# A mixture-of-experts decoder step on one core: a fifth expert weight buffer, separate waits for each weight, and three moved pieces of work

## The chip, the cores and the metric

The kernel runs on one core of a Trainium2 chip. The metric is the time of one execution on the device in microseconds (us). Everything is in 32-bit floating point.

## The reference, cut to what matters

One layer is computed for 320 tokens of width D = 1024: a prompt of 256 tokens and 8 samples of 8 tokens.

```python
xn = rmsnorm(x, norm1);  proj = xn @ w_in
# mixer 1: causal conv + RG-LRU scan       mixer 2: RWKV-7, 16 heads of 64
merged = sigmoid(gate_lru) * out_lru + sigmoid(gate_rwkv) * out_rwkv
x = x + merged @ w_out
# new_shift = P[:, -1]: the last row of the 3360 RWKV columns of each of the 9 sequences is an output
t = rmsnorm(x, norm2)
# router: best of 4 groups, then the best 2 of its 8 experts, softmax weights
h = silu(t @ wg[e]) * (t @ wu[e])          # 32 experts, wg and wu 1024 x 256
y = sum over the two experts of weight * (h @ wd[e])   # wd 256 x 1024
out = rmsnorm(x + y, final_norm)
```

The three matrices of an expert are 1 MB each, so the 32 experts read 100.7 MB. The kernel visits all of them, with at most 64 tokens each (more go to an overflow loop, which does not run here).

## The kernel before, in words

Each engine runs its own program in order; semaphores join them. SP (SyncE) issues nearly all loads, in the order written and each behind its waits.

**Turns.** The two mixers are done in eight turns (`turn(i, first, last)`), one for each pair of heads. TensorE's program in a turn is the chain of the RWKV-7 chunk products: `level_w(k)` and `level_x(k)` for k = 1 to 5, each of which waits for a VectorE step. Between the levels stand halves of the next turn's projections (`ahead`). In the last turn there is no next turn, so only the projection `gl` is left of them, and in the other places TensorE only waits. Single products and projections share two PSUM banks, `bank[0]` and `bank[1]`, alternately: `room` makes TensorE wait until the product two before has been taken by ScalarE or VectorE. The order of these products in a turn is a list (`FULL`, `LAST`).

**Between the turns and the experts.** `out(t)` multiplies by `w_out` for three tiles of tokens; `x2(t)` transposes the normalised rows, and `logits(t)` makes the router's logits (signal `lg_ps`). Then TensorE transposes the 27 chunks of `lastP`, the nine shift-state rows, in groups of four into two banks, and ScalarE copies each group to `rowP` and stores it (lines 904 to 912 and 1229 to 1235). VectorE meanwhile finds group and experts (ending with `Mk`), then waits for ScalarE's exponentials, which stand behind the copies of the shift state, computes the gates (lines 1644 to 1649), waits for TensorE's counts of tokens for each expert (`cnt_ps`, lines 915 to 922), and computes slots and the index lists `gidx` (gather) and `sidx` (scatter). Before the index product TensorE also waits for the last copy of the shift state. GpSimd waits for both lists and starts the gathers of the experts' tokens from `xn2d`.

**Experts.** For each expert TensorE does GU (gate and up, 32 matrix instructions), T (8 transposes of the next expert's gathered tokens), DN (down, of the expert before), and one transpose of the hidden values. Weights lie in four buffers. One semaphore `ew{j}` counts all three loads of buffer j, and GU waits for all three. SP reloads gate and up of a buffer when its GU has ended (`gu`) and down when its DN has ended (`dn`):

```python
with sp.Fori(1, NE // 4) as i:
    for j in range(4):
        weights(j, i * 4 + j, f"ew{j}", i * 4 + (j - 3))
```

Experts 0 to 3 are loaded ahead: 0 and 1 behind the input loads, 2 behind `wo_ps` 3 (the end of `out(2)`), 3 behind the stores of the shift state. On TensorE, ScalarE and VectorE the loop is a first pass of four experts, a hardware loop, and on TensorE and ScalarE a last pass written out. GU also stands behind the arrival of the next expert's gathered tokens.

**End.** SP waits for the last scatter, loads the two results of each token (`ya`, three tiles, two loads each) and, after the first tile's, `final_norm` broadcast to 128 partitions; VectorE combines the tiles and scales them by `final_norm`, ScalarE makes the roots, SP stores.

## Time and profile before

| what | value |
|---|---|
| median of 3 runs | 911.65 us (909.9 to 912.21) |
| the profiled execution | 912.9 us, of which 911.0 us are the span of its trace |
| busy share of the span | PE 88%, PE weight loads 56%, DVE 50%, ACT 28%, POOL 7% |
| turns, `out`, router | 0 to about 618 us |
| experts | about 618 to 884 us |
| end | about 884 to 911 us |
| HBM read | 155.99 MB |

PE is TensorE, DVE is VectorE, ACT is ScalarE, POOL is GpSimd; SPq and ACTq are the queues from which SyncE and ScalarE issue transfers. The busy share of PE is an average over stages with different limits. The granted clock is the share of full speed that TensorE's clock had.

### The profile page before, as it was taken

Reading aid. Unit: us, or ns where it says so; the run is one execution under the profiler, and the core shown is the slowest. Engines: PE = TensorE matmul, PEld = TensorE weight load, DVE = VectorE, ACT = ScalarE, POOL = GpSimd, SP = SyncE. Lnnn points to the kernel's source line nnn. Section 1 sums busy time; section 2 is a strip of 40 time slices with the busy share of each in tenths; the row PEclk is TensorE's granted clock in tenths of the full one; section 3 lists DMA queues with packets and bytes.
Section 4 is the critical chain, followed back from the end, with each engine's and each line's share of the span. In section 5 each row is a group of like instructions: output and inputs, shape, how many; then the busy total and the mean of one; then the engine's idle time right before and its main releaser. Section 6 shows DMA issues by size and latency. Waiting matters only on the chain.

```text
span 911.0 us, 16423 instructions
## 1 busy us (share of the span) xinstructions
PE 800.2 (88%) x6090; PEld 510.3 (56%) x6090; DVE 459.5 (50%) x1067; ACT 250.9 (28%) x585; POOL 66.7 (7%) x74
## 2 busy tenths in 40 slices
PE   3999999999999999999999799957997887877860
PEld 3566666666766666666667564444554554544530
DVE  2476586786785875867867644351111111111115
ACT  4223351441432423514414222321111111111102
POOL 1000000000000000000000000002332222222110
PEclk9999999999999999999999799956999999999995
DMA  9451060250230500602502206755999999999925
GB/s 222 105 145 25 24 170 9 59 140 23 77 98 23 155 20 23 169 7 57 140 23 63 100 26 228 283 218 177 347 393 399 396 398 402 400 391 398 391 80 193
DMA packets 112633, 159.31 MB, mean 175 GB/s; under 512 B 27232, under 2 KB 91290, under 8 KB 104394
## 3 DMA queue, kind: packets, MB, share of 16 engines
q1 hardware_dynamic: 96580, 148.62, 47.3%
q0 software_dynamic: 5296, 6.19, 2.4%
q10 hardware_dynamic: 10727, 4.09, 1.8%
q8 instruction: 20, 0.33, 0.2%
q14 instruction: 10, 0.08, 0.0%
HBM read 155.99 MB, written 13.64 MB: 186 GB/s over the span
## 4 chain that ended last, share of the span: by engine, by line
PE 69%; DMA 17%; DVE 9%; issue 2%; ACT 1%; ACTq 1%; DVEq 0%; SPq 0%; POOL 0%; POOLq 0%
PE bank L591 17%; DMA vecs<-in_exp_down 8%; PE bank L943 8%; DMA wall<-in_exp_down 4%; PE bank L597 4%; PE bank L864 4%; PE bank L950 4%; PE bank L745 4%; PE bank L808 3%; PE bank L693 3%; DMA scratch<-in_exp_down 2%; PE bank L613 2%; PE bank L937 2%; PE bank L700 2%; DVE vecs L1360 2%
## 5 line engine op out<-in xcount | busy, mean ns | idle before, releaser
L591 PE MATMUL bank<-xnT,wall 128*128 128x320 f32 x656 | 197.3, 446 | 1.8 <-DVE wkv L1466 1.8
L591 PEld LDWEIGHTS bank<-xnT,wall 128*128 128x128 f32 x656 | 120.1, 191 | 52.2 <-DVE wkv L1466 5.4
L1705 DVE SCALAR_TENSOR_TENSOR vecs<-vecs,bank 128x128 f32<-128x128 f32 x32 | 9.2, 287 | 160.0 <-ACT vecs L1249 160.0
L943 PE MATMUL bank<-scratch 128*64 128x256 f32 x512 | 58.8, 382 | 19.0 <-DMA scratch<-in_exp_down 9.6
L943 PEld LDWEIGHTS bank<-scratch 128*64 128x64 f32 x512 | 40.3, 137 | 33.0 <-issue 19.8
L1699 DVE COPY vecs<-bank 128x512 f32<-128x512 f32 x32 | 22.1, 691 | 64.1 <-PE bank L950 64.1
L1249 ACT ACTIVATE vecs<-bank 128x128 f32<-128x128 f32 x32 | 8.9, 277 | 148.3 <-PE bank L943 148.3
L497 POOL DMA_INDIRECT merged<-xn2d,gidx x2 | 1.9, 942 | 613.6 <-DVE sidx L1693 613.3
L745 PE MATMUL bank<-xnT,wall 128*128 128x320 f32 x128 | 43.9, 455 | 2.5 <-DVE wkv L1506 2.5
L1459 DVE TENSOR_TENSOR wkv<-bank,consts_sb 128x256 f32<-128x256 f32 (+1 forms) x40 | 18.1, 451 | 48.4 <-PE bank L693 48.4
L943 PE MATMUL bank<-vecs,scratch 128*64 128x256 f32 x256 | 32.3, 409 | 8.8 <-DMA vecs<-in_exp_down 6.5
L943 PE MATMUL bank<-wall,scratch 128*64 128x256 f32 x256 | 31.1, 398 | 10.0 <-DMA wall<-in_exp_down 9.0
L503 POOL DMA_INDIRECT ybuf<-vecs,sidx x32 | 32.1, 1004 | 81.0 <-DVE vecs L1699 81.0
L693 PEld LDWEIGHTS bank<-wkv,scratch 64*64 64x64 f32 x704 | 24.4, 138 | 15.6 <-issue 13.3
L808 PE MATMUL bank<-xnT,wall 128*128 128x320 f32 x112 | 33.1, 439 | 0.0
L693 PE MATMUL bank<-wkv,scratch 64*64 64x64 f32 x704 | 30.0, 228 | 2.0 <-DVE wkv L1466 2.0
L950 PE MATMUL bank<-vecs 128*64 128x512 f32 x128 | 31.0, 605 | 0.4 <-ACT vecs L1256 0.4
L943 PEld LDWEIGHTS bank<-wall,scratch 128*64 128x64 f32 x256 | 21.3, 143 | 17.6 <-issue 11.0
L864 PE MATMUL bank<-wall,merged 128*128 128x512 f32 (+1 forms) x84 | 30.7, 595 | 0.1
L943 PEld LDWEIGHTS bank<-vecs,scratch 128*64 128x64 f32 x256 | 19.8, 147 | 19.0 <-issue 11.5
L1242 ACT ACTIVATE scratch<-bank 128x512 f32<-128x512 f32 x32 | 19.1, 597 | 40.3 <-PE bank L937 40.3
L700 PEld LDWEIGHTS bank<-wkv 64*64 64x64 f32 x576 | 20.2, 139 | 15.3 <-issue 12.7
(374 smaller groups left out, 1376.1 us busy)
## 6 DMA issues: line engine op xcount, KB each, us to landing
wall<-in_w_in SPq DMA_DIRECT2D x58, 512.0 KB, 5.5
vecs<-in_exp_down SPq DMA_DIRECT2D x16, 1024.0 KB, 18.7
scratch<-in_exp_gate SPq DMA_DIRECT2D x16, 1024.0 KB, 16.0
scratch<-in_exp_up SPq DMA_DIRECT2D x16, 1024.0 KB, 20.3
vecs<-in_exp_gate SPq DMA_DIRECT2D x8, 1024.0 KB, 15.5
vecs<-in_exp_up SPq DMA_DIRECT2D x8, 1024.0 KB, 19.9
scratch<-in_exp_down SPq DMA_DIRECT2D x8, 1024.0 KB, 18.3
wall<-in_exp_gate SPq DMA_DIRECT2D x8, 1024.0 KB, 16.3
```

The costliest lines, as they stand in the source:

```text
L503: pool.indirect_dma_start(yhalf, bass.IndirectOffsetOnAxis(ap=e, axis=0), ye[:, b, :], None, bounds_check=4 * QROWS - 1, oob_is_err=False) ...
L591: q = mm(tpbank(L, name), wbuf[name][:, k, :], xnT[:, k, :], start=(k == 0), stop=(k == KC - 1))
L597: mm(tpbank(L, name), lhsT, rhs, start=True, stop=True).then_inc(S("tp"), 1)
L693: q = mm(bank[2][at64(e), 64 * u:64 * u + 64], am[at64(e), u, e, 0, :], X[at64(e), u, :], start=True, stop=True)
L700: q = mm(bank[3][at64(e), 64 * u:64 * u + 64], Y[at64(e), u, :], W[at64(e), u, :], start=True, stop=True)
L745: q = mm(tpbank(L, "gr"), wbuf["gr"][:, k, :], xnT[:, k, :], start=(k == 0), stop=(k == KC - 1))
L808: q = mm(tpbank(L, "lx"), wbuf["lx"][:, k, :], xnT[:, k, :], start=(k == 0), stop=(k == KC - 1))
L864: q = mm(b, merged[:, k, t0:t0 + n], wo[k][:, 512 * h:512 * h + 512], start=(k == 0), stop=(k == KC - 1))
L943: q = mm(b[64 * f:64 * f + 64, 0:256], xT[:, k, :], w[:, :, k, 128 * f:128 * f + 128], start=(k == 0), stop=(k == KC - 1))
L950: q = mm(b[64 * d:64 * d + 64, :], hT[:, 64 * j:64 * j + 64], w[:, j, 512 * d:512 * d + 512], start=(j == 0), stop=(j == 1))
L1242: A(xgT[:, b], bank[b][:].rearrange("p (k s) -> p k s", k=KC), ACT.Copy).then_inc(S("gT"), 1)
L1699: CP(ye[:, j % 2, :], bank[6 + j % 2][:]).then_inc(S("ye"), 1)
```

## The change

- **A fifth buffer.** Five sets of gate and up (`wgu`) and of down (`wdn`, `dn4`) are laid over tiles that are dead at that time. The fifth down matrix lies in three pieces and is loaded by three transfers. Expert 3's gate and up wait for the stores of the shift state alone, expert 4's for the end of `out(2)`. Down of 1 waits for that too, down of 2 for the last `x2` and the stores of `xn2d`, down of 3 and 4 for `lg_ps`.
- **Own waits.** Gate and up of a buffer count on `ewg{b}`, down on `ewd{b}`. GU waits for the first, DN for the second. GU no longer waits for the next expert's tokens; the transposes T do.
- **Loops written out** on SP, TensorE, ScalarE and VectorE.
- **Shift-state rows in the last turn.** The 27 transposes of `lastP` become eight products `rows0` to `rows7` in the list `LAST`: six (four chunks each) at the places between the levels where TensorE only waited, and two (two chunks and one) between the last `level_x(4)` and the product `gx`. ScalarE copies them in between and issues the two stores ahead of the `gx` activation.
- **Gates behind the indices.** VectorE computes the five gate steps after `sidx`. GpSimd's first gathers wait for `gidx` alone.
- **`final_norm`** is loaded before the experts. The rows of the conv and LRU state are copied to another place and stored by eight transfers in place of four.

```diff
-LAST = Products([x for x in TURN if x[0] not in NEXT], AHEAD.order)
+ROWS = [(4 * g, 4 * g + 4) for g in range(6)] + [(24, 26), (26, 27)]
+OWN = [x for x in TURN if x[0] not in NEXT]
+LAST = Products(OWN[:2] + [(f"rows{g}", "a") for g in range(6)] + OWN[2:3] + [("rows6", "a"), ("rows7", "a")] + OWN[3:], AHEAD.order)
...
         wgu = [w.rearrange("p (g k f) -> p g k f", g=2, k=KC) for w in
-               (vecs[:, 0:4096], scratch[:, :], wall[:, 0:4096], scratch3[:, :])]
...
+               (vecs[:, 0:4096], vecs[:, 4096:8192], scratch[:, :], scratch3[:, :], wall[:, 0:4096])]
+        wdn = [scratch2[:, 0:2048], wall[:, 4096:6144], wkv[:, 3 * D:3 * D + 2048], xflat[:, 0:2048], None]
+        dn4 = [wkv[:, 5 * D:6 * D], mflat[:, 2048:2560], xflat[:, 2048:2560]]
...
@@ sync
+            load_gu(0, 0)
+            load_dn(0, 0)
+            load_gu(1, 1)
+            load_gu(2, 2)
+            sp.wait_ge(S("shift_out"), 32)
+            load_gu(3, 3)
             sp.wait_ge(S("wo_ps"), 3)
...
+            load_dn(1, 1)
+            load_gu(4, 4)
+            sp.dma_start(fnb, a["final_norm"].rearrange("(a d) -> a d", a=1).broadcast_to([P, D])).then_inc(S("fn_in"), 16)
+            sp.wait_ge(S("x2T_ps"), 6)
+            sp.wait_ge(S("xn2d"), 48)
+            load_dn(2, 2)
+            sp.wait_ge(S("lg_ps"), 1)
+            load_dn(3, 3)
+            load_dn(4, 4)
+            for e in range(5, NE):
+                sp.wait_ge(S("gu"), e - 4)
+                load_gu(e % 5, e)
+                sp.wait_ge(S("dn"), e - 4)
+                load_dn(e % 5, e)
...
@@ gpsimd
-            pool.wait_ge(S("idx"), 2)
+            pool.wait_ge(S("idx"), 1)
...
@@ tensor, in turn()
                     else:
+                        rows(2 * "rkv".index(n) + half)
                         needs()
+
+                def rows(g):
+
+                    room(L, i, f"rows{g}")
+                    for c in range(*ROWS[g]):
+                        w, at = min(P, RWKV - c * P), P * (c - ROWS[g][0])
+                        q = tr(bank[L.bank(f"rows{g}")][0:9, at:at + w], lastP[0:w, c, :], ident[0:w, 0:w])
+                    q.then_inc(S("tp"), 1)
...
+                if last:
+                    rows(6)
+                    rows(7)
                 pe.wait_ge(S("xc"), i + 1)
...
@@ tensor, experts
+            for e in range(NE + 1):
+                if e < NE:
+                    pe.wait_ge(S(f"ewg{e % 5}"), 32 * (e // 5 + 1))
+                    pe.wait_ge(S("gT"), e + 1)
+                    if e >= 2:
+                        pe.wait_ge(S("h"), e - 1)
+                    GU(bank[2 + e % 2], xgT[:, e % 2], wgu[e % 5]).then_inc(S("gu"), 1)
+                if e + 1 < NE:
+                    n = e + 1
+                    pe.wait_ge(S(f"xg{n % 4}"), 16 * (n // 4 + 1))
+                    T(bank[n % 2], xg[n % 4], n % 4 >= 2).then_inc(S("gT_ps"), 1)
+                if e:
+                    b = (e - 1) % 5
+                    pe.wait_ge(S("hT"), e)
+                    pe.wait_ge(S(f"ewd{b}"), (48 if b == 4 else 16) * ((e - 1) // 5 + 1))
+                    if e >= 3:
+                        pe.wait_ge(S("ye"), e - 2)
+                    DN(bank[6 + (e - 1) % 2], b).then_inc(S("dn"), 1)
+                if e < NE:
+                    pe.wait_ge(S("h"), e + 1)
                     tr(bank[4][:, 0:128], hh, ident).then_inc(S("hT_ps"), 1)
...
@@ scalar, in turn()
+            def rows(L, i, g):
+
+                c0, w = P * ROWS[g][0], min(P * ROWS[g][1], RWKV) - P * ROWS[g][0]
+                tp_ready(act, L, i, f"rows{g}")
+                A(rowP[:, c0:c0 + w], bank[L.bank(f"rows{g}")][0:9, 0:w], ACT.Copy).then_inc(S("taken_a"), 1)
```

## Rows read from the trace of the kernel before

**Rows 1.** The page's slices: GB/s in 40 slices of 22.8 us.

```profile
GB/s 222 105 145 25 24 170 9 59 140 23 77 98 23 155 20 23 169 7 57 140 23 63 100 26 228 283 218 177 347 393 399 396 398 402 400 391 398 391 80 193
```

**Rows 2.** Windows: span, busy us of PE, PEld, DVE, ACT, POOL, clock, DMA share, GB/s.

```profile
750.00:800.00 50.00, 39.61 (x284) 23.70 (x280) 7.60 (x18) 6.91 (x18) 11.03 (x12) 1.00 1.02 399
```

**Rows 3.** Timeline of PE, experts 0, 1, 9 and 31: start, us, work [idle before].

```profile
624.01 6.53 PE L943 MATMUL bank<-vecs,scratch 128*64 128x256 f32 x32 [0.78 <-DMA merged<-xn2d,gidx]
...
632.34 3.67 PE L943 MATMUL bank<-scratch 128*64 128x256 f32 x32 [0.46 <-ACT scratch L1242]
...
688.71 3.67 PE L943 MATMUL bank<-scratch 128*64 128x256 f32 x32 [2.10 <-DMA scratch<-in_exp_down]
...
874.90 3.67 PE L943 MATMUL bank<-scratch 128*64 128x256 f32 x32 [0.92 <-DMA vecs<-in_exp_down]
```

**Rows 4.** The chain that ended last, its end: start, us, what.

```profile
858.09 16.76 DMA vecs<-in_exp_down
...
878.57 1.72 PE bank L950 x8
...
880.97 1.96 PE bank L950 x8
```

**Rows 5.** Timeline of SP's queue: the issue of the last up matrix.

```profile
850.85 0.38 SPq L443 DMA_DIRECT2D scratch<-in_exp_up  x1
```

**Rows 6.** Transfers of 840 to 876 us: issues, KB each, us to landing.

```profile
scratch<-in_exp_up SPq DMA_DIRECT2D x1, 1024.0 KB, 17.7
```

**Rows 7.** Windows in the last turn, columns as in rows 2.

```profile
512.00:514.00 2.00, 0.58 (x18) 0.45 (x15) 1.93 (x5) 0.00 (x0) 0.00 (x0) 0.95 0.00 0
...
522.00:524.00 2.00, 2.00 (x6) 1.15 (x4) 0.00 (x0) 0.00 (x0) 0.00 (x0) 0.50 0.00 0
```

**Rows 8.** Timeline of PE in the last turn.

```profile
511.40 0.80 PE L700 MATMUL bank<-wkv 64*64 64x64 f32 x20 [1.01 <-DVE wkv L1459]
...
515.42 1.33 PE L700 MATMUL bank<-wkv 64*64 64x64 f32 x20 [0.59 <-DVE wkv L1459]
...
520.04 4.38 PE L591 MATMUL bank<-xnT,wall 128*128 128x320 f32 x8
...
524.96 2.42 PE L591 MATMUL bank<-xnT,wall 128*128 128x320 f32 x8
...
527.92 1.40 PE L597 MATMUL bank<-vecs,wxa 128*128 128x320 f32 x4
```

**Rows 9.** Timeline of PE in the router stage.

```profile
597.78 5.62 PE L910 MATMUL bank<-consts_sb,lastP 128*9 128x128 f32 x27
...
604.69 0.97 PE L921 MATMUL bank<-Mk,consts_sb 128*128 128x32 f32 x6
```

**Rows 10.** Timeline of ACT: one copy of a shift-state group.

```profile
598.84 0.59 ACT L1232 ACTIVATE scratch<-bank 9x512 f32<-9x512 f32 x1 [2.97 <-PE bank L910]
```

**Rows 11.** Timeline of DVE in the router stage.

```profile
603.01 0.26 DVE L1642 TENSOR_TENSOR Mk<-OH 128x96 f32<-128x96 f32 x1
606.15 0.17 DVE L1645 TENSOR_REDUCE r<-dg 128x3 f32<-128x12 f32 x1 [2.88 <-ACT r L1239]
...
607.22 0.14 DVE L1652 MEMSET slot<- 128x96 f32 x1
...
617.41 0.18 DVE L1691 CAST gidx<-tokf 64x41 uint32<-64x41 f32 x1
```

**Rows 12.** Timeline of POOL: the first gather.

```profile
618.24 0.96 POOL L497 DMA_INDIRECT merged<-xn2d,gidx  x1 [613.27 <-DVE sidx L1693]
```

**Rows 13.** Windows in the router stage, columns as in rows 2.

```profile
600.00:603.00 3.00, 2.98 (x16) 1.31 (x15) 2.56 (x15) 2.13 (x5) 0.00 (x0) 0.58 0.00 0
603.00:606.00 3.00, 2.66 (x21) 2.14 (x19) 0.26 (x1) 2.32 (x5) 0.00 (x0) 0.99 0.24 40
```

**Rows 14.** Timeline of the end: SP's queue and DVE.

```profile
887.71 0.43 SPq L474 DMA_DIRECT2D vecs<-in_final_norm  x1
...
898.17 1.28 DVE L1736 SCALAR_TENSOR_TENSOR wkv<-wall,r,wkv 128x1024 f32<-128x1024 f32 x1 [3.67 <-DMA scratch<-ybuf]
```

More of the change, by code:

```diff
@@ L437, in dn_src, with load_gu @@
                 return a["exp_down"][0].rearrange("e (j p) d -> p e j d", p=P)[:, bass.ds(e, 1)].rearrange("p e j d -> p (e j) d")
[L439 to L441 removed]
+            def load_gu(b, e):
                 for g, name in enumerate(("exp_gate", "exp_up")):
[L443 to L446 removed]
@@ L448, in _ @@
-            weights(0, 0, "ew0")
-            weights(1, 1, "ew1")
-            sp.wait_ge(S("wo_ps"), 3)
-            weights(2, 2, "ew2")
-            sp.wait_ge(S("shift_out"), 32)
-            sp.wait_ge(S("rows_out"), 64)
-            weights(3, 3, "ew3")
-            with sp.Fori(1, NE // 4) as i:
-                for j in range(4):
-                    weights(j, i * 4 + j, f"ew{j}", i * 4 + (j - 3))
+                    sp.dma_start(wgu[b][:, g].rearrange("p k f -> p (k f)"), gu_src(name, e)).then_inc(S(f"ewg{b}"), 16)
@@ new lines, in load_dn @@
+            def load_dn(b, e):
+                if b < 4:
+                    sp.dma_start(wdn[b].rearrange("p (j d) -> p j d", j=2), dn_src(e)).then_inc(S(f"ewd{b}"), 16)
+                else:
+                    for j, c0, c1, t in ((0, 0, D, dn4[0]), (1, 0, 512, dn4[1]), (1, 512, D, dn4[2])):
+                        sp.dma_start(t, a["exp_down"][0, e, j * P:j * P + P, c0:c1]).then_inc(S("ewd4"), 16)
+            load_gu(0, 0)
+            load_dn(0, 0)
+            load_gu(1, 1)
+            load_gu(2, 2)
@@ L464, in _ @@
                     sp.wait_ge(S("dn"), j + NE)
-                    weights(0, e, "ew0")
+                    load_gu(0, e)
+                    load_dn(0, e)
                 sp.wait_ge(S("y_out0"), 8 * NE + 16 * NOV)
@@ L507, in _ @@
                 if e < NE:
-                    if e == 2:
-                        pool.wait_ge(S("lg_ps"), 1)
                     if e >= 4:
@@ L718, in turn @@
                     level_x(k)
+                if last:
+                    rows(6)
+                    rows(7)
                 pe.wait_ge(S("xc"), i + 1)
@@ L976, in _ @@
-            pe.wait_ge(S("xg0"), 16)
-            T(bank[0], xg[0]).then_inc(S("gT_ps"), 1)
-            experts(0, True, False)
-            with pe.Fori(1, NE // 4 - 1) as i:
-                experts(i, False, False)
-            experts(NE // 4 - 1, False, True)
-            pe.wait_ge(S("hT"), NE)
-            pe.wait_ge(S("ye"), NE - 2)
-            DN(bank[7], wdn[3]).then_inc(S("dn"), 1)
+                        q = mm(b[64 * d:64 * d + 64, :], hT[:, 64 * j:64 * j + 64], down(w, j, d), start=(j == 0), stop=(j == 1))
@@ L1118, in turn @@
                 A(tu[:], tu[:], ACT.Tanh, scale=0.7978845608028654).then_inc(S("tu"), 1)
+                if last:
+                    for g in range(6):
+                        rows(L, i, g)
                 if not last:
@@ L1125, in turn @@
                 A(tgl[:], tpbank(L, "gl"), ACT.Tanh, scale=0.5).then_inc(S("taken_a"), 1)
+                if last:
+                    rows(L, i, 6)
+                    rows(L, i, 7)
+                    taken(act, L, i, "rows7")
+                    for dst, src in ((o["shift_p"][0], rowP[0:1, 0:RWKV]), (o["shift_s"][0], rowP[1:9, 0:RWKV])):
+                        act.dma_start(dst, src).then_inc(S("shift_out"), 16)
                 tp_ready(act, L, i, "gx")
@@ L1242, in xcols @@
                 A(xgT[:, b], bank[b][:].rearrange("p (k s) -> p k s", k=KC), ACT.Copy).then_inc(S("gT"), 1)
-            def experts(i, first, last):
-                for j in range(4):
-                    act.wait_ge(S("gu"), i * 4 + (j + 1))
-                    if not (first and j == 0):
-                        act.wait_ge(S("h"), i * 4 + j)
-                    A(th, bank[2 + j % 2][:, 0:128], ACT.Tanh, scale=0.5).then_inc(S("th"), 1)
-                    if not (last and j == 3):
-                        act.wait_ge(S("gT_ps"), i * 4 + (j + 2))
-                        xcols((j + 1) % 2)
-                    if not (first and j == 0):
-                        act.wait_ge(S("dn"), i * 4 + j)
-                    act.wait_ge(S("hT_ps"), i * 4 + (j + 1))
-                    A(hT, bank[4][:, 0:128], ACT.Copy).then_inc(S("hT"), 1)
             act.wait_ge(S("gT_ps"), 1)
             xcols(0)
-            experts(0, True, False)
-            with act.Fori(1, NE // 4 - 1) as i:
-                experts(i, False, False)
-            experts(NE // 4 - 1, False, True)
+            for e in range(NE):
+                act.wait_ge(S("gu"), e + 1)
+                if e:
+                    act.wait_ge(S("h"), e)
+                A(th, bank[2 + e % 2][:, 0:128], ACT.Tanh, scale=0.5).then_inc(S("th"), 1)
+                if e + 1 < NE:
+                    act.wait_ge(S("gT_ps"), e + 2)
+                    xcols((e + 1) % 2)
+                if e:
+                    act.wait_ge(S("dn"), e)
+                act.wait_ge(S("hT_ps"), e + 1)
+                A(hT, bank[4][:, 0:128], ACT.Copy).then_inc(S("hT"), 1)
             act.wait_ge(S("ov"), 1)
```

142 lines of the change are left out of this document (51 added, 91 removed).

## The prediction

> **What bounds the kernel now.** I read the page's slices first. The transfer rate [rows 1] is low and ragged through the turns (7 to 170 GB/s in most slices), where weights arrive long before they are used. It stands at 391 to 402 GB/s from slice 30 on until the last weights are in. So the turns are bound by the engines and the experts by transfers. The window of 50 us in the middle of the experts [rows 2] says the same: the 16 transfer engines were busy all the time (share 1.02, 399 GB/s), while TensorE was busy 39.6 of 50 us at full clock.
>
> The timeline of TensorE [rows 3] gives the two paces. From expert 1 (632.34) to expert 9, without the 2.10 us that expert 9 waited, eight experts took 54.3 us, 6.78 us each: there TensorE set the pace, living on the four sets loaded ahead. From expert 9 (688.71) to expert 31 (874.90), 22 experts took 186.2 us, 8.46 us each: there the transfers set it. The first reload is allowed by the end of GU of expert 0, at 624.01 + 6.53 = 630.5. From then on 28 sets have to come, and their end is the end of the stage. What precedes 630.5 is a chain through the last turn, `out`, and the router. What follows the last landing is a short chain [rows 4]: from 858.09 + 16.76 = 874.85, GU 3.67, DN of expert 30 1.72, a transpose and a copy, DN of expert 31 until 880.97 + 1.96 = 882.93. Then come scatter, reload and norms, 28 us.
>
> **The fifth buffer.** One set more is in before the first reload, so 27 sets come after it. One set costs 8.46 us of the transfer-bound stretch [rows 3]: gain 8.5. Bounds: 7.9 (its 3.15 MB alone at 399 GB/s [rows 2]) and 8.7, which is 28 sets over the 244.3 us from 630.5 to 874.85. Is the fifth set really in by then? The slices from 569 to 638 us show 283, 218 and 177 GB/s [rows 1], about half of what the queue reaches; 3 MB take 8 us, and the last of their waits, `lg_ps`, comes at 597.8 [rows 9], 26 us ahead of GU 0. TensorE does not become the bound: at 6.78 us it would be through GU 31 some 28 us before its weights. The stores of the state rows, four small transfers more on ScalarE's queue, lie beside `out(1)`: nothing.
>
> **Own waits.** In the middle of the stage the transfers set the pace, and an earlier GU gives nothing. At its end GU 31 and DN 30 (3.67 + 1.72 us) can run while the last down matrix still arrives. How much earlier are gate and up in? A set takes 8.46 us, a third of it 2.8 us. I take 2.8 us. The view of transfers seems to say more: the last up matrix, issued at 850.85 [rows 5], is given 17.7 us to landing [rows 6], 868.6, 6.3 us before the down matrix. But all three loads of a buffer count on one semaphore, so this moment is a count and not a matrix. If it were the matrix, everything up to DN 31 would be hidden and the gain would be 6.0 us (882.93 against 874.85 + 2.0). I keep that as the far bound.
>
> The Trainium skill ("DMA: Bandwidth & Descriptors", Why a DMA increments its semaphore by 16 and not by 1) says that with two transfers in flight on one semaphore an intermediate value does not tell which bytes have landed. By that page the 2.8 us stand, by the row read plainly 6.0 us.
>
> **The end.** `final_norm` is issued between the tiles' loads [rows 14], 0.43 us of SP's queue, and its 0.5 MB stand ahead of the second tile: 1.3 us at 399 GB/s. VectorE waited 3.67 us for that tile [rows 14]. The gain lies between 1.3 and 3.7; since both the issue and the bytes go, I take 2.0. Loading it earlier costs 0.5 MB at a time with room [rows 1].
>
> **The shift-state rows, where they go.** They add 27 transposes. In the router stage these took 5.62 us [rows 9], 0.21 us each, at a clock of 0.50 to 0.58 [rows 13]; so a group of four is about 0.85 us at half clock and 0.45 at full. The places are gaps in which TensorE waits for VectorE: 1.01 and 0.59 us are two of them [rows 8]. At full clock six groups fit into the gaps, at half clock three of them overrun by 0.3 us each. ScalarE has nothing else there; one copy takes 0.59 us [rows 10] and `room` wants it only two groups later. The last two groups are different: `gx` (527.92 [rows 8]) now waits for the copy of `rows6`, behind three transposes: 0.35 us of transposes and 0.35 us of a copy of half the width, a cost of 0.7 us on the path. The two store issues on ScalarE delay the activation of `gx`, which VectorE does not need before the level ends: nothing.
>
> What else happens there is larger. TensorE was busy 0.58 of 2 us at 512 to 514, and the clock fell from full (2.4 GHz) to half (1.2 GHz); it was still at 0.50 at 522 to 524 [rows 7]. In that stretch the same level product took 1.33 us against 0.80, and the first half of `gl` took 4.38 us where the second took 2.42 [rows 8]. Four level products at half clock cost about 1.9 us too much, `gl` 2.0 us. With the transposes TensorE works nearly through these gaps, so I take it that the clock holds: 3.9 us back, less 0.7, makes 3.2 us of gain. Bounds: 3.9 of gain; and 0.7 + 0.9 = 1.6 us of loss if the clock falls all the same.
>
> **The shift-state rows and gates, where they leave.** VectorE waited 2.88 us for ScalarE's exponentials and then did five gate steps before it reached the slots at 607.22 [rows 11]. Without them it waits for the counts alone. These ended at 605.66 [rows 9], so at first sight 1.4 us are gained. But the counts ran at full clock (0.99), to which it had risen while the transposes ran (a mean of 0.58 over 600 to 603, so full from about 602.5 on) [rows 13]. Now TensorE would stand idle from 597.8 to 603.3, and the clock stays at half. The counts took from 603.3 to 605.66, 2.3 us; times 4.38 / 2.42 that is 4.2 us, and the slots start at 607.6, 0.4 us later than before. Waiting for `gidx` alone saves the last two steps of VectorE, about 0.35 us of the 0.65 between the end of `gidx` at 617.59 and the gather at 618.24 [rows 11, 12]. GU 0 no longer waits for the second gather, 0.1 us at most, since its own tokens were transposed and copied only just before. Together nothing: 0.0, with 1.9 us of gain as one bound (counts at full clock) and 0.4 us of loss as the other. The gates themselves are done during the gathers.
>
> The Trainium skill ("TensorE: Matmul & The Clock Gate", Part 4: PE-mode transpose) says that transposes do not count as busy for the clock in the way that matmuls do. Here the clock rose behind a run of transposes [rows 13], which speaks against it. By that page the router would gain 1.9 us, and the last turn would lose 1.6.
>
> **Written-out loops.** No wait in the rows belongs to a loop's turn. I take nothing.
>
> **The sum.** 3.2 (last turn) + 0.0 (router) + 8.5 (buffer) + 2.8 (own waits) + 2.0 (end) = 16.5 us. The profiled execution's span of 911.0 becomes 894.5, its time of 912.9 becomes 896.4. It was 1.25 us above the median, so on the median the forecast is 911.65 - 16.5 = 895.2, say 895.
>
> **Rivals.**
> - *The clock falls in the last turn although the gaps are filled.* For it: four transposes fill 0.45 us of a gap of up to 1.4 us. 1.6 us of loss in place of 3.2 of gain: 900. Chance 0.22.
> - *Transposes keep no clock up*, as a mechanism of this kernel: the rise at 602.5 had another cause and comes without them too. The last turn loses 1.6, the router gains 1.9: 911.65 + 1.6 - 1.9 - 8.5 - 2.8 - 2.0 = 898. Against it: the rise itself [rows 13]. This is what the page on the clock gate would give. Chance 0.10.
> - *The fifth set gives nothing*, because the rate per set falls as much as is loaded ahead (more in flight, the down matrix in three pieces of shorter rows): 895.2 + 8.5 = 904. Against it: the transfer engines are busy all the time, with bytes that stay the same. Chance 0.06.
> - *Slower: the instructions of the written-out loops come late.* They come over the same transfer engines, busy all the time [rows 2], and 20 more experts are read from memory instead of from a loop. TensorE has 8.46 - 6.78 = 1.7 us to spare for each. It decides from (16.5 / 20) + 1.7 = 2.5 us of stall for each expert; with 4 us it would be 895 + 20 x 2.3 = 941. Against it: experts 28 to 31 are written out already, and expert 31 started 0.05 us after its last landing [rows 3, 4]. Chance 0.05.
> - The forecast, clock held and all other terms near their values: 0.57.
>
> Range: 888 to 901. The low end has the far bounds of the own waits and of the end together with some of the router's; the high end takes in the clock falling. About 2 in 10 are left out, the 904 and the slower case among them. A measurement of this kernel tells about 0.3%, 2.7 us, from no change. Faster 0.92, same 0.03, slower 0.05.
>
> **What would show it.** In the profile after: TensorE's clock at full through the last turn, `gl`'s first half at 2.4 us; `gx` 0.7 us later behind the level before it; the counts at half clock, with VectorE waiting for TensorE at `slot`; the first gather at the same distance behind `lg_ps`; the last down landing 27 x 8.46 + 7.4 = 236 us behind the end of GU 0 (before: 28 x 8.46 + 7.4 = 244.3); GU 31 ended before that landing or about 1 us behind it; the second tile's combination about 2 us nearer to the scatter. The prediction fails most easily at the clock, which I infer from one fall and two rises, and at the transfer rate with five sets, of which nothing here is measured.

## The result, and the profile after

The changed kernel took 900.52 us (median of 4 runs, 898.15 to 900.87), the kernel before 911.93 on the same chip. The ratio is 0.9865, 95% interval [0.9846, 0.9884]: 1.35%, or 12.3 us, faster. The interval reaches from 10.6 to 14.0 us, and the two medians alone differ by 11.4. The forecast was 16.5 us. The profiled execution's span is 898.5 us, against 911.0. One execution of all kernels, the profiled one of h_warm below, took 1144.3 us at a mean clock of 0.66; it is in no ratio, and h_warm has no trace here.

I compare the two traces between landmarks that both have. First the slices of the page, GB/s in 40 slices of 22.5 us, to be held against [rows 1]:

```profile
GB/s 225 80 136 62 25 167 14 26 173 8 54 142 23 73 104 23 138 39 23 166 12 46 142 30 117 407 342 124 341 378 385 390 389 397 392 385 397 398 151 175
```

Two slices (407 and 342) now carry the sets loaded ahead. In the stage that the transfers bound, the nine slices from the 30th on have a mean of 390, where it was 396 before. Five sets ahead are there; the rate behind them is lower.

The last turn, timeline of TensorE (start, us, work, idle before it), to be held against [rows 8], and two windows to be held against [rows 7]:

```profile
509.66 0.66 PE L690 MATMUL bank<-consts_sb,s0raw 128*128 128x128 f32 x4
510.16 0.60 PE L708 MATMUL bank<-consts_sb,lastP 128*9 128x128 f32 x4
...
515.37 0.80 PE L723 MATMUL bank<-wkv,scratch 64*64 64x64 f32 x20 [0.88 <-DVE wkv L1489]
516.10 0.61 PE L708 MATMUL bank<-consts_sb,lastP 128*9 128x128 f32 x4
...
519.97 2.42 PE L612 MATMUL bank<-xnT,wall 128*128 128x320 f32 x8
...
525.90 0.51 PE L708 MATMUL bank<-consts_sb,lastP 128*9 128x128 f32 x3
526.84 1.32 PE L618 MATMUL bank<-vecs,wxa 128*128 128x320 f32 x4 [0.43 <-ACT scratch L1103]
...
549.13 12.28 PE L899 MATMUL bank<-wall,merged 128*128 128x512 f32 x28
```

```profile
512.00:514.00 2.00, 1.52 (x31) 1.05 (x27) 1.89 (x6) 1.52 (x4) 0.00 (x0) 1.00 0.04 12
522.00:524.00 2.00, 2.00 (x22) 1.38 (x21) 0.42 (x1) 0.00 (x0) 0.00 (x0) 1.00 0.00 0
```

The granted clock is 1.00 where it was 0.95 and then 0.50. The first half of `gl` takes 2.42 us instead of 4.38, level products 0.80 instead of 1.33. `gx` waits 0.43 us for the copy of `rows6`. From the transposes of the wkv state (509.66) to the start of `out(0)` (549.13) there are 39.47 us. In the kernel before it was 42.38, between these two:

```profile
507.91 0.66 PE L669 MATMUL bank<-consts_sb,s0raw 128*128 128x128 f32 x4
...
550.29 12.28 PE L864 MATMUL bank<-wall,merged 128*128 128x512 f32 x28
```

Gain 2.9. A group of four transposes takes 0.60 us at full clock; the prediction had 0.45.

The router, timelines of TensorE, VectorE and GpSimd, to be held against [rows 9, 11, 12]:

```profile
602.14 0.63 PE L945 MATMUL bank<-Mk,consts_sb 128*128 128x32 f32 x2 [5.47 <-DVE Mk L1665]
...
604.48 1.62 PE L947 MATMUL bank<-Mk,consts_sb 128*128 128x32 f32 x6
...
622.43 5.05 PE L969 MATMUL bank<-vecs,scratch 128*64 128x256 f32 x32 [0.78 <-ACT scratch L1271]
```

```profile
606.19 0.14 DVE L1668 MEMSET slot<- 128x96 f32 x1 [4.10 <-PE bank L947]
```

```profile
616.76 0.96 POOL L518 DMA_INDIRECT merged<-xn2d,gidx  x1 [611.79 <-DVE gidx L1707]
```

VectorE waits 4.10 us for the counts, which run at half clock from 602.14 to 606.10, 4.0 us (at full clock they took 2.3). From `out(0)` to GU of expert 0 there are 73.3 us against 73.7. GU 0 itself took 5.05 us against 6.53. The first gather starts 20.1 us behind the end of the logits (596.67); before it was 20.4.

The end of the expert stage, timeline of TensorE, then the issues of the last two matrices on SP's queue, then their times to landing (us, last column), to be held against [rows 3 to 6]:

```profile
864.54 3.67 PE L969 MATMUL bank<-vecs,scratch 128*64 128x256 f32 x32 [0.96 <-DMA vecs<-in_exp_up]
868.05 1.89 PE L976 MATMUL bank<-scratch,vecs 128*64 128x512 f32 x8
...
870.62 1.94 PE L976 MATMUL bank<-wall,vecs 128*64 128x512 f32 x8 [0.43 <-ACT vecs L1286]
```

```profile
844.01 1.99 SPq L450 DMA_DIRECT2D vecs<-in_exp_up  x1
846.05 0.97 SPq L454 DMA_DIRECT2D wall<-in_exp_down  x1
```

```profile
vecs<-in_exp_up SPq DMA_DIRECT2D x1, 1024.0 KB, 20.5
wall<-in_exp_down SPq DMA_DIRECT2D x1, 1024.0 KB, 21.0
```

With a semaphore of its own for gate and up and one for down, the landing times of the two that come last are those of matrices: the last up matrix is in at 844.01 + 20.5 = 864.5, where GU 31 starts; the last down matrix at 846.05 + 21.0 = 867.05. That is 2.55 us later, and DN 31 at 870.62 waits only for ScalarE. Now the length of the stage: from the end of GU 0 (627.48) to the last landing there are 239.6 us. The forecast said 236 (235.8 before rounding). From the end of GU 0 to the start of GU 31 there are 237.06 us, before 244.36: 7.3 gained of 11.3 forecast.

The end, VectorE, to be held against [rows 14]:

```profile
885.66 1.28 DVE L1750 SCALAR_TENSOR_TENSOR wkv<-wall,r,wkv 128x1024 f32<-128x1024 f32 x1 [1.68 <-DMA scratch<-ybuf]
```

The wait for the second tile is 1.68 us (3.67 before). From the first issue of the results' loads to this combination there are 9.16 us, before 11.31. The two first issues, SP's queue, the kernel before and the changed one:

```profile
886.86 0.34 SPq L472 DMA_DIRECT2D wall<-ybuf  x1
```

```profile
876.50 0.34 SPq L495 DMA_DIRECT2D wall<-ybuf  x1
```

The pair of executions adds up: the turns before the last one started 1.75 us later (below), then 2.9 in the last turn, 0.4 in the router, 1.5 in GU 0, 7.3 in the experts and 2.15 at the end: 12.5 us, the difference of the spans.

### The profile page after: what moved, and what is told of

Read it like the earlier page. It is cut to its first block, busy times and chain, and to the rows that moved or that the text cites. A ratio compares the mean times of both kernels' runs of the same rounds, so it can differ in the third digit from the quotient of the medians.

```text
span 898.5 us, 16125 instructions
## 1 busy us (share of the span) xinstructions
PE 801.6 (89%) x6090; PEld 503.7 (56%) x6090; DVE 459.7 (51%) x1067; ACT 250.8 (28%) x586; POOL 66.7 (7%) x74
## 4 chain that ended last, share of the span: by engine, by line
PE 66%; DMA 13%; DVE 9%; SPq 7%; issue 2%; ACT 1%; ACTq 1%; DVEq 0%; POOLq 0%
PE bank L612 17%; DMA scratch<-in_exp_up 9%; PE bank L969 5%; SPq L450 5%; PE bank L618 4%; PE bank L899 4%; PE bank L780 4%; PE bank L843 3%; PE bank L976 3%; PE bank L723 3%; DMA vecs<-in_exp_up 2%; PE bank L634 2%; PE bank L730 2%; DVE vecs L1383 2%; PE bank L590 2%
## 5 line engine op out<-in xcount | busy, mean ns | idle before, releaser
L969 PE MATMUL bank<-vecs,scratch 128*64 128x256 f32 x448 | 56.2, 408 | 11.2 <-DMA vecs<-in_exp_up 10.0
L969 PE MATMUL bank<-scratch 128*64 128x256 f32 x384 | 45.8, 393 | 7.7 <-DMA scratch<-in_exp_up 7.7
L969 PEld LDWEIGHTS bank<-vecs,scratch 128*64 128x64 f32 x448 | 33.9, 147 | 29.5 <-DMA vecs<-in_exp_up 11.5
L518 POOL DMA_INDIRECT merged<-xn2d,gidx x4 | 3.7, 920 | 612.7 <-DVE gidx L1707 611.8
L963 PEld LDWEIGHTS bank<-consts_sb,merged 64*128 64x128 f32 x256 | 30.7, 200 | 17.2 <-issue 17.2
L969 PEld LDWEIGHTS bank<-scratch 128*64 128x64 f32 x384 | 27.3, 141 | 22.7 <-DMA scratch<-in_exp_up 9.1
L963 PE MATMUL bank<-consts_sb,merged 64*128 64x64 f32 x256 | 35.1, 278 | 5.2 <-DMA merged<-xn2d,gidx 5.2
L520 POOL DMA_INDIRECT merged<-xn2d,gidx x28 | 26.6, 948 | 114.5 <-PE bank L963 114.5
L969 PE MATMUL bank<-wall,scratch 128*64 128x256 f32 x192 | 23.7, 403 | 6.8 <-DMA wall<-in_exp_up 6.8
```

What stands on the lines that cost most here:

```text
L520: pool.indirect_dma_start(xg[j], None, xn2d, bass.IndirectOffsetOnAxis(ap=e, axis=0), bounds_check=last, oob_is_err=False).then_inc(S(sem) ...
L963: q = tr(b[:, CAP * k:CAP * k + CAP], src[:, k:D:KC], ident[r, r])
L969: q = mm(b[64 * f:64 * f + 64, 0:256], xT[:, k, :], w[:, :, k, 128 * f:128 * f + 128], start=(k == 0), stop=(k == KC - 1))
```

## The experiments

Each run's profile was read at the same landmarks. *Last turn* is from the wkv state's transposes to `out(0)`; *stage* from the end of GU 0 to GU 31; *end* from the first issue of the results' loads to the second combination. Times in us.

| kernel | ratio to before, 95% interval | last turn | stage | end |
|---|---|---|---|---|
| before | 1 | 42.38 | 244.36 | 11.31 |
| changed | 0.9865 [0.9846, 0.9884] | 39.47 | 237.06 | 9.16 |
| c_unroll | 1.0002 [0.9986, 1.0018] | 42.35 | 245.01 | 9.75 |
| b_own | 0.9975 [0.9961, 0.9989] | 42.38 | 243.74 | 10.46 |
| l_clock | 0.9961 [0.9943, 0.9978] | 38.60 | 244.46 | 9.68 |
| d_four | 0.9958 [0.9941, 0.9975] | 39.47 | 245.42 | 8.43 |
| e_split | 0.9897 [0.9876, 0.9917] | 39.46 | 239.09 | 9.57 |
| j_throttle | 0.9866 [0.9845, 0.9888] | 39.47 | 237.18 | 8.40 |
| g_gates | 0.9861 [0.9838, 0.9884] | 39.47 | 236.93 | 8.86 |
| k_one | 0.9856 [0.9835, 0.9877] | 39.48 | 235.64 | 8.63 |
| m_joint | 0.9879 [0.9862, 0.9896] | 39.47 | 239.45 | 8.72 |
| f_norm | 0.9873 [0.9852, 0.9894] | 39.48 | 237.75 | 11.47 |
| h_warm | 0.9836 [0.981, 0.9862] | none | none | none |
| n_best | 0.9814 [0.9789, 0.984] | 39.47 | 236.61 | 8.18 |

The first turn's wkv transposes start anywhere from 70.1 to 73.8 us in these profiles, and in four executions of the same code up to there (kernel before, c_unroll, b_own, l_clock) at 70.4, 70.1, 72.9 and 73.8. The eight other profiles of changed kernels start the last turn's transposes between 507.75 and 511.06 us, the four of unchanged turns between 507.63 and 511.33. So the 1.75 us lost ahead of the last turn in the profiled pair lie within this scatter.

**l_clock: the kernel before, with idle transposes in the last turn's gaps.**

```diff
                     elif not last:
                         proj(L, i, n, i + 1, 4 * half, 4 * half + 4, needs)
                     else:
+                        if not (n == "r" and half == 0):
+                            for c in range(4):
+                                tr(bank[6][0:9, P * c:P * c + P], lastP[:, c, :], ident)
                         needs()
```

> The kernel before, with four idle transposes into a free bank at five of the six places between the levels of the last turn, copied by nobody; the shift-state rows stay in the router stage. Theory: what the last turn gained is the clock. From the turn's transposes of the wkv state to the first product of out the changed kernel takes 39.5 us against 42.4 before; without the wait of gx (0.7 us) this one should take 38.6 to 38.9, and the whole be 3.5 us faster than before. Rival (transposes keep no clock up): the clock falls as before, 42.4 us or more, and the whole is 0 to 1.5 us slower.

```profile
517.03 0.80 PE L696 MATMUL bank<-wkv,scratch 64*64 64x64 f32 x20 [0.88 <-DVE wkv L1469]
517.76 0.60 PE L681 MATMUL bank<-consts_sb,lastP 128*9 128x128 f32 x4
...
521.63 2.42 PE L591 MATMUL bank<-xnT,wall 128*128 128x320 f32 x8
```

```profile
512.00:514.00 2.00, 1.40 (x43) 1.29 (x44) 1.93 (x8) 1.56 (x6) 0.00 (x0) 1.00 0.03 8
```

Added work made the kernel 3.6 us faster. The last turn took 38.60 us, 3.8 less than in the kernel before; nothing else there was changed. So the gain is the clock, at its full level of 2.4 GHz, and transposes between the levels keep it there. The changed kernel's last turn is 0.87 us longer than this: that is what the last groups of transposes ahead of `gx` and its wait cost (forecast 0.7).

**g_gates: the changed kernel, with VectorE's five gate steps back ahead of the slots.**

```diff
+            dve.wait_ge(S("gexp"), 2)
+            step(RED(col(3), dg[:], AX.X, ADD))
...
             dve.wait_ge(S("cnt_ps"), 1)
```

> The changed kernel with the five gate steps back ahead of the slots. Theory: VectorE waits 4 us for the counts at half clock there, the five steps take 1.1 us and hide in that wait: no change, 900.5. Rival (moving the gates is what shortened the router stage): 1.1 us slower.

```profile
600.74 0.17 DVE L1672 TENSOR_TENSOR r<-r 128x3 f32<-128x3 f32 x1
604.19 0.14 DVE L1675 MEMSET slot<- 128x96 f32 x1 [3.29 <-PE bank L947]
```

The counts start at 600.07 and VectorE reaches the slots 4.12 us later, against 4.05 (602.14 to 606.19). The five steps only shorten its wait, from 4.10 to 3.29 us. Moving them saves nothing as long as the counts come last.

**c_unroll: the kernel before with the expert loops written out; b_own: that, and own semaphores with four buffers.** In b_own GU also no longer waits for the next expert's tokens, as in the changed kernel, so it tests both waits together.

```diff
-            with pe.Fori(1, NE // 4 - 1) as i:
+            for i in range(1, NE // 4 - 1):
...
-                sp.dma_start(wdn[j], dn_src(e)).then_inc(S(sem), 16)
+                sp.dma_start(wdn[j], dn_src(e)).then_inc(S(d_sem), 16)
```

> The kernel before with the expert loops written out on the four engines and nothing else. In the changed kernel a set takes 8.68 us where the transfers set the pace, against 8.57 before. Theory A (instructions): the extra instructions, fetched by the same transfer engines, are what makes a set dearer; this kernel then has about 8.68 us for each set between experts 13 and 28 and is 2 to 3 us slower than the kernel before. Theory B (short rows of the fifth down matrix) and theory C (more sets in flight): the pace here stays at 8.57 and the time is that of the kernel before.

> As the kernel with the loops written out, and own semaphores for gate and up and for down; four buffers. The forecast's term: GU of expert 31 starts when gate and up are in, a third of a set before the down matrix, so 2.8 us faster than the kernel with the loops alone. Rival, by the landing row read plainly: 6.0 us faster. Rival: 0, if the last transfers are reordered so that gate and up come in last with the rest.

The loops alone change the time by 0.2 us of 912, with 1.5 us of uncertainty to each side: the slower rival is out, and so are theory A's 2 to 3 us. By the ratios b_own is 0.27%, 2.5 us, faster than c_unroll. Its last two weights, issues and times to landing:

```profile
850.68 2.31 SPq L444 DMA_DIRECT2D scratch<-in_exp_up  x1
...
857.93 0.38 SPq L447 DMA_DIRECT2D vecs<-in_exp_down  x1
```

```profile
scratch<-in_exp_up SPq DMA_DIRECT2D x1, 1024.0 KB, 24.1
vecs<-in_exp_down SPq DMA_DIRECT2D x1, 1024.0 KB, 19.4
```

The last up matrix landed at 850.68 + 24.1 = 874.8, where GU 31 starts; the last down matrix at 857.93 + 19.4 = 877.3, 2.55 us behind it, as in the changed kernel. The stage of the one profile shows less: 243.74 against 245.01, 1.3 us.

**m_joint: the changed kernel, with GU waiting for its own down matrix too.**

```diff
                     pe.wait_ge(S(f"ewg{e % 5}"), 32 * (e // 5 + 1))
+                    pe.wait_ge(S(f"ewd{e % 5}"), (48 if e % 5 == 4 else 16) * (e // 5 + 1))
```

> The changed kernel, but GU of an expert also waits for its own down matrix, as in the kernel before; five buffers and everything else stay. Theory: in the changed kernel the last up matrix landed at 864.5 and the last down matrix at 867.05, 2.55 us behind it, and GU 31 ran in between. GU 31 now starts 2.55 us later: stage 239.6 in place of 237.06, time 2.5 us more. Rival 'a third of a set hides elsewhere' (the chain behind, with the scatter and the reload of the results, waits for something else): the stage is 2.5 us longer, the time less than 1 us. Rival by the far bound of the forecast (the whole of DN 30 and GU 31 hidden): 5 to 6 us more.

```profile
866.83 3.67 PE L969 MATMUL bank<-vecs,scratch 128*64 128x256 f32 x32 [0.95 <-issue]
```

GU 31 starts 239.45 us behind the end of GU 0 (627.38), 2.4 later; up to the first load of the results the distance stays 2.4 longer (251.4 us behind the end of GU 0, against 249.0). The ratio rose by 0.0014 against the changed kernel's and by 0.0023 against k_one's on the same chip, 1.3 to 2.1 us, with intervals that overlap. The time alone does not settle it; the trace says about 2.4 us, not 5 to 6.

**d_four: the changed kernel with only four sets ahead.**

```diff
-            load_gu(4, 4)
...
-            load_dn(4, 4)
-            for e in range(5, NE):
-                sp.wait_ge(S("gu"), e - 4)
+            for e in range(4, NE):
+                sp.wait_ge(S("gu"), e - 3)
```

> The changed kernel with only four sets ahead: expert 4's weights wait for GU and DN of expert 0, and so on; everything else as in the changed kernel. The forecast's term: one set more after the first reload, 8.5 us slower than the changed kernel, about 909. Theory C (more in flight makes a set dearer, 8.68 instead of 8.57): the pace goes back to 8.57 and the loss is only 28 x 8.57 - 27 x 8.68 = 5.6 us, about 906. Theories A and B: the pace stays at 8.68 and the loss is 8.7.

```profile
620.77 6.56 PE L967 MATMUL bank<-vecs,scratch 128*64 128x256 f32 x32 [0.78 <-ACT scratch L1269]
...
872.75 3.67 PE L967 MATMUL bank<-vecs,scratch 128*64 128x256 f32 x32 [0.96 <-DMA vecs<-in_exp_up]
```

The stage is 245.42 us, 8.4 longer than in the changed kernel; by the ratios the time is 8.5 us longer. The fifth set is worth what one set costs, and theory C's 5.6 us are out. But if the last down matrix comes 2.55 us behind the start of GU 31, as in the changed kernel, 28 sets now need 248 us, where the kernel before needed 244.3 with the same number ahead. So the loss of pace does not come from loading a fifth set ahead.

**j_throttle: the changed kernel, from expert 10 on reloading one expert later.**

```diff
-                sp.wait_ge(S("gu"), e - 4)
+                sp.wait_ge(S("gu"), e - (3 if e >= 10 else 4))
...
-                sp.wait_ge(S("dn"), e - 4)
+                sp.wait_ge(S("dn"), e - (3 if e >= 10 else 4))
```

> The changed kernel, in which from expert 10 on a reload waits for one expert more, so that no more sets are in flight than with four buffers, while five are loaded ahead. If the number in flight makes a set dearer (8.68 us against 8.55), its pace goes back to 8.55 to 8.6 from expert 14 on, and it is 1.5 to 2 us faster than the changed kernel. If not, the pace stays and one set fewer stands ahead: no more than 0 to 8 us slower, depending on whether the transfers are ever left without work; with work always queued, 900.5.

Stage and time are unchanged (237.18 against 237.06, 0.9866 against 0.9865). What is queued a set deeper neither helps in mid-stage nor takes from the rate.

**e_split: all down matrices in three transfers; k_one: the fifth in one, into a tile of its own.**

```diff
+                    for j, c0, c1 in ((0, 0, D), (1, 0, 512), (1, 512, D)):
+                        sp.dma_start(wdn[b][:, D * j + c0:D * j + c1], a["exp_down"][0, e, j * P:j * P + P, c0:c1]).then_inc(S(f"ewd{b}"), 16)
```

```diff
+        dn5 = sb("dn5", [P, 2048])
...
-        wdn = [scratch2[:, 0:2048], wall[:, 4096:6144], wkv[:, 3 * D:3 * D + 2048], xflat[:, 0:2048], None]
+        wdn = [scratch2[:, 0:2048], wall[:, 4096:6144], wkv[:, 3 * D:3 * D + 2048], xflat[:, 0:2048], dn5[:, :]]
```

> The changed kernel with every down matrix loaded by three transfers (4 KB rows, twice 2 KB rows), as the fifth buffer's is. Theory B (short rows): the cost of one set in five now falls on every set; if it explains the 0.11 us for each set, a set now takes about 8.57 + 5 x 0.11 = 9.1 us and the kernel is 12 us slower than the changed one. Theories A and C: no change, 900.5 us.

> The changed kernel with the fifth down matrix in a tile of its own (2048 columns), loaded by one transfer in place of three. In the changed kernel the stage from the end of GU 0 to the start of GU 31 is 237.06 us and the pace of a set 8.68 to 8.72 us, against 8.60 to 8.64 with the loops written out alone. Theory 'three pieces': splitting all the other down matrices cost 2.0 us in the stage (239.09) and 2.9 us by the ratios, for about 22 sets of 27; the fifth's five sets cost a quarter to a fifth of that, so the stage becomes about 236.6 and the time falls by 0.5 us, which the ratio can hardly tell. Theory 'where the five sets lie' (mixed tiles of the fifth buffer cost more than the short rows themselves): the pace returns to 8.62 and the time falls by 1.8 us. Rival 'neither': stage 237.0, pace 8.68 or more; then the rest of the loss of pace lies with what the written-out programs read, or stays open.

Single starts of GU are uneven, so here I read what passed in a fixed stretch, 700 to 840 us, in which the transfers bind every kernel: the queue of weights' packets, their MB and their share of the 16 engines' time. Looped (l_clock), loops written out (c_unroll), changed and e_split, in this order (q1 carries the weights, q8 and q14 instructions; packets, MB, share):

```profile
q1 hardware_dynamic: 9403, 52.78, 95.9%
...
q14 instruction: 1, 0.01, 0.0%
```

```profile
q1 hardware_dynamic: 9397, 52.69, 95.6%
...
q8 instruction: 7, 0.11, 0.3%
q14 instruction: 4, 0.03, 0.1%
```

```profile
q1 hardware_dynamic: 9774, 51.94, 95.7%
```

```profile
q1 hardware_dynamic: 11723, 51.34, 96.0%
```

The share hardly moves and the MB fall: the same engine time carries less. Here are all profiles, MB of weights in the stretch:

| kernels | MB |
|---|---|
| loops, four buffers (before, l_clock) | 53.07, 52.78 |
| loops written out, four buffers (c_unroll, b_own) | 52.69, 52.82 |
| changed, d_four, j_throttle, m_joint, f_norm, g_gates | 51.94, 52.17, 51.84, 51.93, 52.17, 52.09 |
| fifth down matrix in one transfer (k_one, n_best) | 52.46, 52.16 |
| all down matrices in three (e_split) | 51.34 |

The means are 52.9, 52.75, 52.0, 52.3 and 51.3. On the 228 us that 27 sets take, the step from 52.9 to 52.0 is 1.7%, 3.9 us: all of what the stage fell short of the forecast. Two kernels of one row differ by up to 0.6% themselves, so the smaller steps are estimates. The written-out loops have 0.3% (0.7 us), with about 0.14 MB of instruction packets, 0.4% of the engines' time, where the looped kernel has 0.01 MB. The three pieces have about 0.6% (1.3 us): k_one's stage is 1.6 and n_best's 0.6 us below the mean of the four changed kernels with three pieces and all five sets (237.06, 237.18, 236.93, 237.75). In e_split, splitting the other four costs 1.3%, 3.0 us, or 0.75 for each buffer, 2.0 us in its one stage and 2.9 us by the ratios. Theory B had put 12 us on it, so short rows explain only a small part of the dearer set. By time alone k_one can't be told from the changed kernel.

The single packets recorded in the traces, in the same 140 us, say where the rest lies. Gate and up come in packets of 8 KB, down in 4 KB, in the split matrices also 2 KB. "Beside" means that a packet of GpSimd's gathers and scatters (q0) ran at the same time on any of the 16 engines.

| packets | before, l_clock | c_unroll, b_own | changed, d_four, j_throttle, m_joint, f_norm, g_gates |
|---|---|---|---|
| 8 KB of gate and up, mean ns | 328, 328 | 329, 331 | 333 to 335 |
| the same, no gather or scatter packet beside them | 315, 315 | 315, 315 | 315 |
| the same, one beside them | 342, 341 | 343, 342 | 345 to 350 |
| 4 KB of down, mean ns | 170, 170 | 169, 168 | 168 to 169 |
| 2 KB of down, mean ns | none | none | 90 to 94 |

Two packets of 2 KB take 180 to 188 ns where one of 4 KB takes 169; for the fifth buffer's five sets this makes some 0.6 us, the low end of the estimate above. A packet of gate or up with no gather or scatter beside it costs the same in all these kernels. What rose is the time of those that have one beside them, and mostly their share (49, 50, 52 and 60% in the first four kernels, 52 to 62% in the changed ones). k_one and n_best, with every down matrix in one transfer, read the same: 334 and 335 ns, 314 alone, 346 and 348 beside. From written-out loops to the changed kernels this is 4 ns on the mean, and 256 such packets for each of 27 sets over 16 engines make some 1.7 us, an estimate.

**f_norm: the changed kernel with `final_norm` loaded in the end again.**

> The changed kernel with the load of final_norm back between the first and the second tile's loads of the end. Theory: 1.3 us for its 0.5 MB at 399 GB/s and up to 0.4 us of SP's queue ahead of the second tile: from the first issue of the results' loads to the second combination 10.3 to 11 us in place of 8.4 to 9.6 us, time 1.4 to 2.2 us more. Rival 'the end is paced by VectorE' (three combinations of about 1.3 us and the norms between them): the second combination moves, the last does not, and the time is the same within 0.5 us.

```profile
876.63 0.43 SPq L496 DMA_DIRECT2D wall<-in_final_norm  x1
```

```profile
887.24 1.29 DVE L1751 SCALAR_TENSOR_TENSOR wkv<-wall,r,wkv 128x1024 f32<-128x1024 f32 x1 [3.90 <-DMA scratch<-ybuf]
```

The second combination comes 11.47 us behind the first issue, against 8.2 to 9.6 in the eight other profiles of changed kernels, and the third follows it at the same 3.9 us as there. So the load did hold up the whole end, by 1.9 to 3.3 us in this execution. The four kernels with the load in its old place that were derived from the kernel before show 9.7 to 11.3. From the mean of those (10.3) to the mean of the eight (8.7) there are 1.6 us. The ratio rose by 0.0008 to 0.0017 (against the changed kernel's and k_one's), which its interval does not tell from nothing.

**h_warm and n_best: idle matrix instructions in the router stage; n_best with k_one's tile.** In both, 6 of them stand ahead of the wait for `Mk`, 12 ahead of the index product and 9 ahead of the first gathered tokens (a trace counts each of these calls twice, so the 12 are its x24):

```diff
+            def warm_up(m):
+                for _ in range(m):
+                    mm(bank[4][:, 0:256], ident, consts[:, 0:256], start=True, stop=True)
```

> The changed kernel with idle products (128x128 by 128x256, into a free bank) while TensorE waits in the router stage: 6 ahead of Mk, 12 ahead of the index product, 9 ahead of the first gathered tokens. Theory: the half clock costs 1.7 us at the counts, 1 us at the index product and 1.4 to 2.9 us at GU of expert 0, and all of it delays the first reload, so about 4 to 5 us faster than the changed kernel, near 896. Rival: the idle products overrun their gaps and give back what the clock gains: 900 or more. Rival: a first reload that is earlier gives nothing, since the transfers are late anyway: 900.5.

> A candidate to beat both kernels: the changed kernel with 6, 12 and 9 idle matrix instructions in the router stage, which are to keep TensorE's clock up through the counts, the index product and the first expert, and with the fifth down matrix in one transfer. The idle instructions alone gave 897.84 us against 912.7 (ratio 0.9836), without a usable trace. Theory: the counts, 4.0 us from Mk to cnt_ps in the changed kernel, take 2.4 us, and GU 0 runs 5.0 us or less; from out(0) to the end of GU 0 about 76 us in place of 78.4 to 79.4; with the one transfer a ratio of 0.981 to 0.983. Rival: the clock falls all the same while VectorE searches the experts (597.8 to 602), since six instructions end long before, and only the product behind it gains: 0.5 us, ratio 0.985.

h_warm took 897.84 us (897.5 without its one long execution), n_best 896.41, the lowest of all. n_best's interval lies just below the changed kernel's, but against k_one on the same chip (2.9 us slower by the medians) the intervals overlap. The trace of n_best, TensorE, and two windows (span, busy us of PE, PEld, DVE, ACT, POOL, clock, DMA share, GB/s):

```profile
600.93 0.41 PE L951 MATMUL bank<-Mk,consts_sb 128*128 128x32 f32 x2 [0.92 <-DVE Mk L1673]
...
603.77 8.13 PE L943 MATMUL bank<-consts_sb 128*128 128x256 f32 x24
...
620.32 6.61 PE L976 MATMUL bank<-vecs,scratch 128*64 128x256 f32 x32 [0.78 <-ACT scratch L1279]
```

```profile
600.00:603.00 3.00, 2.08 (x17) 1.95 (x16) 0.81 (x5) 0.21 (x1) 0.00 (x0) 0.90 0.86 318
603.00:606.00 3.00, 3.00 (x9) 2.49 (x9) 1.79 (x11) 0.00 (x0) 0.00 (x0) 0.50 1.03 416
```

The counts took 2.9 us in place of 4.0, but the clock fell to half during the idle instructions behind them, and again for GU 0 (6.61 us; 0.50 over 621 to 624 us). From `out(0)` to the end of GU 0 this execution needed 79.6 us, the eight profiles of changed kernels without idle instructions show 78.4 to 80.1: no gain. It was one of the kernel's slower ones. The five executions go in the order of their mean clock: 898.4 and 899.9 us at 0.967, 896.4 at 0.970, 895.7 at 0.972, 893.4 at 0.976, where k_one's five stood at 0.959 to 0.963. So a shorter time goes with a higher clock; where in those executions the clock held, no trace shows, and the gain of the idle instructions stays unexplained.

## Why the prediction was right, and where its sizes were off

The measured 900.52 us lie in the range of 888 to 901, by half a microsecond, and 4.2 us of the forecast 16.5 did not come. The time alone would have fitted the rival in which the clock falls (900) better than the forecast. It is the traces that show the clock held and that the loss lies elsewhere: that the range still took it in, by room left for another reason, is luck.

- **Last turn, 3.2 forecast, 2.9 measured.** Clock 3.8 (forecast 3.9), the transposes and the wait ahead of `gx` 0.87 (0.7). Both rivals about the clock are out. The Trainium skill ("TensorE: Matmul & The Clock Gate", Part 4: PE-mode transpose) says that transposes do not count as busy in the same way. l_clock speaks against it for this kernel: transposes were the only thing added, and the clock stayed full (1.00 over 512 to 514 us). The measurement decides.
- **Router, 0.0 forecast, 0.4 measured in the pair**, which is less than the scatter between profiles (72.3 to 74.2 us from `out(0)` to GU 0). The counts fell to half clock without the transposes ahead of them, 4.0 us against 4.2 forecast, and this ate what VectorE's freed wait would have given. GU 0 took 5.0 to 6.6 us among the profiles of all kernels, by the moment at which the clock rose; the pair's 1.5 us there are scatter: from `out(0)` to the end of GU 0 the mean of four profiles without the change is 79.6, of eight with it 79.1.
- **Fifth buffer, 8.5 forecast, 8.4 to 8.5 measured** (d_four).
- **Own waits, 2.8 forecast, 2.4 to 2.55 measured** (m_joint, the two landings, the ratios of b_own; 1.3 by b_own's stage). The far bound of 6.0 took a moment of the shared count for a landing. The Trainium skill ("DMA: Bandwidth & Descriptors", Why a DMA increments its semaphore by 16 and not by 1) says that such a moment does not tell which bytes are in, and here the traces agree: the shared count put the last up matrix 6.3 us ahead of the down matrix, own semaphores show 2.55.
- **End, 2.0 forecast, 1.6 by the means**, 2.15 in the pair, 1.9 to 3.3 in f_norm.
- **The term that failed: the cost of a set.** The prediction had "27 x 8.46 + 7.4 = 236 us behind the end of GU 0", with the loops at "I take nothing", and it argued that "the transfer engines are busy all the time, with bytes that stay the same". They were as busy, and the weights' bytes were the same, but each byte cost 1.7% more engine time: 239.6 us, 3.8 more than 27 x 8.46 + 7.4. About 0.7 belong to the written-out loops and 0.6 to 1.3 to the fifth down matrix in three pieces with shorter rows (estimates). The remaining 1.9 to 2.6 are in d_four and j_throttle too, so it is not the number of sets ahead or in flight. b_own has 52.82 MB, so it is not the own semaphores either. That it lies with the places of the five sets in memory is only an argument; no run moved the gate and up tiles, and the packets speak against it, since alone they cost the same in all. The extra time arises where gate and up meet gathers and scatters. Why they met at a higher price in the changed kernels, no run shows; the tiles of the gathered tokens moved as well, from two to one. The rival "the fifth set gives nothing" had named a fall of the rate, at 8.5 us and a chance of 0.06. The rate did fall, by less than half of that, and what it gave as one reason, more in flight, is not it.

The sum by the means is 2.9 + 0.4 + 7.3 + 1.6 = 12.2 us, against 12.3 measured. The interval of the measurement is 1.7 us to each side, so an agreement this close is chance.

## What to carry to other kernels

When transfers bind a stage, one more buffer was worth one set (8.4 us), but leave room for a set to become dearer: a busy share of 1.02 says that the engines have no idle time, not that a byte costs the same after a change. Read MB of one queue in a fixed stretch to see it; starts of instructions are too uneven. Then compare packets of one size, with and without another queue's beside them. And before moving work out of TensorE's idle places, look at the granted clock of what stands behind them: cheap transposes in gaps were worth 3.8 us here, and taking others away cost the counts 1.6.

## What the runs showed of the hardware that I had not expected

- Issuing a 1 MB transfer took SP's queue up to 7.3 us, where [rows 5] show 0.38. In the timeline of SP's queue, changed kernel:

```profile
750.82 0.43 SPq L454 DMA_DIRECT2D scratch<-in_exp_down  x1
751.30 7.31 SPq L450 DMA_DIRECT2D vecs<-in_exp_gate  x1
```

  Landing of 1 MB took 21 to 27 us (medians of 700 to 840 us) in place of 17 to 21. Most of this is not the fifth set: b_own, with four, has 21 to 26 us as well and issues of up to 5.8 us, where c_unroll, with the shared semaphore, has 17 to 22 and up to 2.8. It cost nothing that the runs show: j_throttle, with less queued, had the same stage.
- An 8 KB packet of weights took 315 ns alone and 341 to 350 ns beside a packet of a gather or scatter, in the table of the single packets above.
- In n_best the clock fell to half at 603 to 606 us while TensorE was busy for 3.00 of 3.00 us, having worked 2.08 of the 3 us before. So idle instructions behind the counts did not hold the clock in this execution.
